# One core: the last two expert blocks in another order, second outputs fetched by adding gathers, and VectorE's order behind them

## Chip, cores and metric
One core of one Trainium2 chip. The metric is the device time of one execution in microseconds; the time of a kernel is the median of its runs.

## What is computed
One layer of a token mixer with a mixture-of-experts feed-forward on 512 latent tokens of width 2048 (and 256 context tokens). Only its last part matters here:

```
h   = rmsnorm(x2, norm2_w) * (1 + m4) + m3                # x2: tokens after the mixer
two experts of 16 per token, gates g0, g1, tokens sorted by expert into blocks of 128
y_b = (silu(h_b @ w1[e]) * (h_b @ w3[e])) @ w2[e]         # per block of 128 slots, times the gate
f[t]   = y[dest_0[t]] + y[dest_1[t]]
out[t] = rmsnorm(x2[t] + m5 * f[t], final_norm_w)
```

w1 and w3 are 2048 x 512 per expert, w2 is 512 x 2048.

## The kernel before, in words
All products are of float32 data, split into a high and a low part. A **unit** is half a 1 MB weight load: 128 x 1024 weights. For each unit ScalarE converts the high part (`e_hi`), VectorE subtracts it (`e_lo`), and TensorE makes six matmuls of 128 x 128 by 128 x 512 (`e_unit`, L1060 to L1070). Six raw buffers (`e_raw`) and six split ones (`e_hi`, `e_lo`) go round. Semaphore `e_units` counts finished units (six ahead), `e_split` the split ones, so ScalarE converts unit u when unit u-6 is done, and SyncE loads into a raw buffer when both its units are split (`load_e`, L621).

One block of the mixture has 24 units: eight up units for w1 into PSUM bank 0, eight for w3 into bank 1, eight down units for w2 into banks 2 to 5 (`up_unit`, `down_unit`). Between them stand the sigmoid (`sig1`, ScalarE), `silu` and `gate_up` (VectorE), four transposes of the gated activation (`turn_act`, TensorE) and the split of its transpose (`act_hi` on ScalarE, `act_lo` on VectorE, into `actT_hi` and `actT_lo`). The down products' result is scaled by the gates and copied to `y_sb` by ScalarE (`y_copy`, L1528), and GpSimd stores it in two halves into `block_outputs` in HBM (`store`, L2555 on).

The blocks are staggered: a turn of the loop makes the w1 units of block e, the w3 units of block e and the down units of block e-1. Blocks are numbered 0 to 15 (LAST = 15), and there were no extra blocks with these inputs. **The last turn** is written out by hand (L1137 to L1159): eight w1 units of block 15 (u = 0 to 7, with block 14's `turn_act` behind u = 2), eight down units of block 14 (u = 8 to 15), eight w3 units of block 15 (u = 16 to 23), then 16 small transposes, `turn_act(LAST)` and the eight down units of block 15 (u = 24 to 31). The list of loads (L642 on) and the loops of ScalarE (L1575 on) and VectorE (L2282 on) follow that order, each with the other work between chosen units. `AHEAD` is 5, so `u == AHEAD + 17` is u = 22. Block 15's outputs never go to HBM: ScalarE scales them into `v_last`, VectorE multiplies them by `m5_row`, and TensorE spreads them to their tokens by a one-hot matrix (`slots_last`) into PSUM. For token tiles 0 and 1 it first adds x2 there with an identity matrix (L1186), for tiles 2 and 3 a DMA adds x2 to `y_buf`.

**The outputs of blocks 0 to 14** come back by token: for each tile i of 128 tokens, `gather_y(z, i, ...)` (L2597) is an indirect DMA of 128 rows of 8 KB, z = 0 for the first expert of the token and z = 1 for the second. GpSimd issues them in this order once block 14's store has landed: (0,0) into `y_buf0`, (1,0) into `y_pair`, (0,1), (0,2), (0,3), then its own addition of `y_pair` into `y_buf0` (L2611), then the adding gathers (1,1), (1,2), (1,3), each behind the landing of its (0,i). Then it adds x2 of tiles 2 and 3 by DMA (L2620).

**VectorE's tail** (L2337 on) works on these: `modulate_y(i)` multiplies `y_buf i` by `m5_row`; `whole(i)` adds `y_buf i` and PSUM in two halves into x2; ScalarE then squares and sums the row (L1612); `finish(i)` takes the mean, waits for ScalarE's root, and multiplies by the reciprocal and `final_norm_w` (L2331). SyncE sends each tile out. The order is: four pieces of `v_last`, modulate 0, modulate 1, whole 0, modulate 2, modulate 3, whole 1, finish 0, finish 1, whole 2, whole 3, finish 2, finish 3.

Of the kernel before, what the change touches and what calls it, by code (L numbers as in the profile page):

```python
# [23 lines left out]
F32 = mybir.dt.float32  # L24
# [3 lines left out]
ALU = mybir.AluOpType  # L28
# [4 lines left out]
P = 128  # L33
D = 2048
# [3 lines left out]
NTOK = SEQ // P  # L38
NCTX = CTX // P
HEADS = 8  # L40
# [92 lines left out]
def build(nc, x, c, ctx_tokens, c_ctx, w_ada, b_ada, norm1_w, norm2_w, w_in, w_pool_group, pool_scale,  # L133
# [22 lines left out]
    with stack:  # L156
# [187 lines left out]
        y_buf = [Room(nc, base, at, at + 8).new(f"y_buf{i}", [P, D], F32) for i, at in enumerate((162, 98, 106, 10))]  # L344
        y_pair = Room(nc, base, 170, 178).new("y_pair", [P, D], F32)
        slots_last = Room(nc, base, 202, 204).new("slots_last", [P, NTOK, P], F32)
# [34 lines left out]
        def bank(b, n=512):  # L381
# [73 lines left out]
            [sem(f"y_in{i}") for i in range(NTOK)], sem("f_sum"), sem("o_rdy"), sem("o_out"))  # L455
        v_gated, v_out, slots_rdy, last_mm, y_mod, y_joined, USED = (
            c_sig_f, ff_taken, c_kgT_rdy, c_v_T, c_v_ev, c_kg_b, HEADS)
        y3_in, Y3_IN = rows_in, 7 * 16

# [53 lines left out]
        def _(sp):  # L513
# [112 lines left out]
            def piece(e, n):  # L626
                w, k, rows = (w_e1_d, n, 4) if n < 4 else (w_e3_d, n - 4, 4) if n < 8 else (w_e2_d, n - 8, 1)
                return w[ds(e, 1), :, rows * k:rows * k + rows, :].rearrange("o p k n -> (o p) (k n)")
# [16 lines left out]
            for i in range(16):  # L645
                load_e(L_LAST + i, (L_LAST + i) % EP,
                       piece(LAST - 1, 4 + i) if 4 <= i < 8 else piece(LAST, i if i < 4 else i - 4))
            sp.wait_ge(table_rdy, 1)
# [20 lines left out]
        def _(pe):  # L669
# [467 lines left out]
            pe.wait_ge(u_rdy, LAST)  # L1137
            for u in range(8):
                if u % 2 == 0:
                    pe.wait_ge(xe_rdy, LAST * 4 + (u // 2 + 3))  # L1140
                up_unit(G_LAST + u, (G_LAST + u) % EH, u, 0)
                if u == 2:
                    turn_act(LAST - 1)
            pe.wait_ge(actT_rdy, LAST + 2)
            pe.wait_ge(y_ev, LAST * 4)
            for u in range(8, 16):
                down_unit(G_LAST + u, (G_LAST + u) % EH, u - 8)
            pe.wait_ge(act_rdy, LAST)
# [50 lines left out]
        def _(act_e):  # L1199
# [375 lines left out]
            for u in range(AHEAD, 29):  # L1575
                last_hi(u)
                if u == AHEAD + 3:
                    act_hi(LAST - 1)
                if u == AHEAD + 9:
                    act_e.wait_ge(e_units, G_LAST + EH + 8)  # L1580
                    sig1(LAST)
                if u == AHEAD + 17:
                    y_copy(LAST - 1, LAST - 1, G_LAST + EH + 16)
            act_hi(LAST)
# [35 lines left out]
        def _(dve):  # L1620
# [661 lines left out]
            for u in range(AHEAD, 29):  # L2282
                last_lo(u)
                if u == AHEAD + 3:
                    act_lo(LAST - 1)
                if u == AHEAD + 9:
                    silu(LAST)
# [46 lines left out]
            def modulate_y(i):  # L2334
                tt(y_buf[i][:], y_buf[i][:], m5_row[:], ALU.mult).then_inc(y_mod, 1)

            for n in range(4):  # L2337
                cols = slice(n * 512, (n + 1) * 512)
                dve.wait_ge(v_gated, USED + n + 1)
                tt(v_last[:, cols], v_last[:, cols], m5_row[:, cols], ALU.mult).then_inc(v_out, 1)  # L2340
            dve.wait_ge(y_joined, USED + 1)
            modulate_y(0)
            dve.wait_ge(y_in[1], 16)
            modulate_y(1)
            dve.wait_ge(y_mod, USED + 1)
            whole(0)
            dve.wait_ge(y_in[2], 16)
            modulate_y(2)
            dve.wait_ge(y_in[3], 16)
            modulate_y(3)  # L2350
            dve.wait_ge(y_mod, USED + 2)
            whole(1)
            finish(0)
            finish(1)
            dve.wait_ge(y_in[2], 32)
            whole(2)
            dve.wait_ge(y_in[3], 32)
            whole(3)
            finish(2)
# [4 lines left out]
        def _(pool):  # L2364
# [238 lines left out]
            gather_y(0, 0, y_buf[0]).then_inc(y_in[0], 16)  # L2603
            gather_y(1, 0, y_pair).then_inc(y_in[0], 16)
            pool.wait_ge(e_split, 2 * EP + G_LAST + 24)
            gather_y(0, 1, y_buf[1]).then_inc(y0_in[0], 16)
            gather_y(0, 2, y_buf[2]).then_inc(y0_in[1], 16)
            pool.wait_ge(e_units, EH + G_LAST + 24)
            gather_y(0, 3, y_buf[3]).then_inc(y3_in, 16)
            pool.wait_ge(y_in[0], 32)  # L2610
            tt(y_buf[0][:], y_buf[0][:], y_pair[:], ALU.add).then_inc(y_joined, 1)  # L2611
            pool.wait_ge(y0_in[0], 16)
            gather_y(1, 1, y_buf[1], ALU.add).then_inc(y_in[1], 16)
            pool.wait_ge(y0_in[1], 16)
            gather_y(1, 2, y_buf[2], ALU.add).then_inc(y_in[2], 16)
            pool.wait_ge(y3_in, Y3_IN + 16)
            gather_y(1, 3, y_buf[3], ALU.add).then_inc(y_in[3], 16)
            for i in (2, 3):
# [57 lines left out]
```

## Time and profile before

| | |
|---|---|
| median of 3 runs | 2256.38 us (2256.22 to 2256.63) |
| the profiled execution | 2258.2 us |
| its span | 2256.6 us |
| mean granted clock of TensorE | 0.984 |
| busy: TensorE, VectorE, ScalarE, GpSimd | 96%, 69%, 44%, 24% |
| moved by DMA | 533.45 MB, mean 236 GB/s |

Times in the rows are microseconds from the start of the span, durations are microseconds too. A timeline row that merges several instructions (x4) gives the start of the first and their busy time together; in brackets stands how long the engine was idle before and what released it. The chain of waits follows the end of the program back to what released each step. PE is TensorE, DVE VectorE, ACT ScalarE, POOL GpSimd, SPq the DMA queue of SyncE, POOLq that of GpSimd.

### The profile page before, as it was taken

To read this page: it belongs to the slowest core of one execution; us is meant where nothing else is said; L and a number is where in the kernel's file an instruction comes from. 1 tells how busy PE (TensorE), PEld (TensorE's weight loads), DVE (VectorE), ACT (ScalarE), POOL (GpSimd) and SP (SyncE) were. 2 spreads that over 40 slices of the span, in tenths; PEclk is the share of its full clock that TensorE was granted. 3 is DMA by queue.
4 is the path that set the end of the run, shared out by engine and by line. 5 is a ranking of instruction groups with operands and counts; after the bars stand their busy time and mean duration, and the time that the engine had idled before them with its cause. 6 is when DMAs were issued, how large, how long until landed. Compare 5 with 4: busy or idle time off the path is not lost.

```text
span 2256.6 us, 36440 instructions
## 1 busy us (share of the span) xinstructions
PE 2162.3 (96%) x12376; PEld 1764.9 (78%) x12376; DVE 1552.2 (69%) x1941; ACT 992.4 (44%) x1216; POOL 536.3 (24%) x673
## 2 busy tenths in 40 slices
PE   4889999999999999999999999999799999999996
PEld 2679878888887887788888888788688888888883
DVE  3468555676567656766666766743688989889886
ACT  3334333333233324322222222332268888888882
POOL 0046435453554354111111111100000010110102
PEclk9989999999999999999999999999899999999998
DMA  9965462232222233677677666834499999999998
GB/s 388 390 208 156 149 217 79 85 93 80 83 86 84 83 89 96 214 225 248 213 226 248 218 222 207 273 128 148 171 385 407 416 415 421 417 418 418 418 377 258
DMA packets 327823, 533.45 MB, mean 236 GB/s; under 512 B 12464, under 2 KB 253616, under 8 KB 297808
## 3 DMA queue, kind: packets, MB, share of 16 engines
q1 hardware_dynamic: 294048, 393.91, 49.0%
q0 software_dynamic: 33712, 138.71, 17.6%
q8 instruction: 39, 0.64, 0.1%
q14 instruction: 24, 0.20, 0.0%
HBM read 493.74 MB, written 36.73 MB: 235 GB/s over the span
## 4 chain that ended last, share of the span: by engine, by line
PE 80%; DVE 4%; issue 2%; DMA 2%; POOL 1%; ACT 0%; DVEq 0%; POOLq 0%; ACTq 0%
PE ps L715 13%; PE ps L717 12%; PE ps L716 12%; PE ps L1070 7%; PE ps L1068 7%; PE ps L1069 7%; PE ps L946 3%; PE ps L947 3%; PE ps L948 3%; PE ps L1005 2%; PE ps L1007 2%; PE ps L1006 2%; PE ps L1094 1%; PE ps L825 1%; DMA y_buf<-block_outputs,dest_i 1%
## 5 line engine op out<-in xcount | busy, mean ns | idle before, releaser
L1666 DVE TENSOR_TENSOR w_lo<-raw,w_hi 128x1024 fp32r<-128x1024 f32 x272 | 349.1, 1283 | 357.1 <-ACT w_hi L1229 355.5
L1229 ACT CAST w_hi<-raw 128x1024 fp32r<-128x1024 f32 x272 | 285.1, 1048 | 584.6 <-PE ps L717 277.2
L715 PE MATMUL ps<-hl_hi,w_hi 128*128 128x512 f32 x1280 | 505.9, 395 | 3.6 <-DVE hl_lo L1732 1.4
L717 PE MATMUL ps<-hl_hi,w_lo 128*128 128x512 f32 x1280 | 498.8, 390 | 0.0
L716 PE MATMUL ps<-hl_lo,w_hi 128*128 128x512 f32 x1280 | 498.7, 390 | 0.0
L2121 DVE TENSOR_TENSOR e_lo<-e_raw,e_hi 128x1024 fp32r<-128x1024 f32 x357 | 421.5, 1220 | 44.1 <-ACT e_hi L1510 36.8
L1510 ACT CAST e_hi<-e_raw 128x1024 fp32r<-128x1024 f32 x357 | 369.1, 1058 | 72.6 <-PE ps L1070 72.4
L715 PEld LDWEIGHTS ps<-hl_hi,w_hi 128*128 128x128 f32 x1280 | 240.4, 188 | 54.7 <-issue 3.4
L717 PEld LDWEIGHTS ps<-hl_hi,w_lo 128*128 128x128 f32 x1280 | 240.3, 188 | 50.8
L716 PEld LDWEIGHTS ps<-hl_lo,w_hi 128*128 128x128 f32 x1280 | 240.5, 188 | 47.8
L1068 PE MATMUL ps<-e_hi,xe_hi 128*128 128x512 f32 x512 | 201.2, 393 | 0.1
L1070 PE MATMUL ps<-e_hi,xe_lo 128*128 128x512 f32 x512 | 199.5, 390 | 0.0
L1069 PE MATMUL ps<-e_lo,xe_hi 128*128 128x512 f32 x512 | 199.3, 389 | 0.0
L1952 DVE SCALAR_TENSOR_TENSOR ada_acc<-ada,silu_c,ada_acc 128x512 f32<-128x512 f32 x240 | 180.2, 751 | 12.1 <-DMA ada<-in_w_ada 5.3
L2559 POOL DMA_DIRECT2D block_outputs<-y_sb x30 | 16.2, 540 | 467.7 <-ACT y_sb L1533 460.9
L1070 PEld LDWEIGHTS ps<-e_hi,xe_lo 128*128 128x128 f32 x512 | 96.1, 188 | 20.3
L1068 PEld LDWEIGHTS ps<-e_hi,xe_hi 128*128 128x128 f32 x512 | 96.4, 188 | 19.5 <-DVE xe_lo L2225 0.3
L1069 PEld LDWEIGHTS ps<-e_lo,xe_hi 128*128 128x128 f32 x512 | 96.2, 188 | 19.4
L1068 PE MATMUL ps<-e_hi,actT_hi 128*128 128x512 f32 x256 | 105.4, 412 | 1.4 <-DVE actT_lo L2244 1.4
L1005 PE MATMUL ps<-w_hi,m_hi 128*128 128x512 f32 x256 | 100.7, 393 | 1.6 <-DVE m_lo L1971 1.6
L1070 PE MATMUL ps<-e_hi,actT_lo 128*128 128x512 f32 x256 | 101.4, 396 | 0.0
L1069 PE MATMUL ps<-e_lo,actT_hi 128*128 128x512 f32 x256 | 100.6, 393 | 0.0
(388 smaller groups left out, 3588.5 us busy)
## 6 DMA issues: line engine op xcount, KB each, us to landing
e_raw<-in_w_e SPq DMA_DIRECT2D x192, 1024.0 KB, 9.6
raw<-in_w_in SPq DMA_DIRECT2D x208, 512.0 KB, 3.9
ada<-in_w_ada POOLq DMA_DIRECT2D x64, 1024.0 KB, 6.4
ada_ring<-in_w_ada SPq DMA_DIRECT2D x32, 1024.0 KB, 14.2
raw<-in_w_out SPq DMA_DIRECT2D x32, 512.0 KB, 4.0
block_outputs<-y_sb POOLq DMA_DIRECT2D x30, 512.0 KB, 6.7
block_outputs<-osq POOLq DMA_DIRECT2D x1, 8192.0 KB, 27.8
raw<-in_w_branch_hgrn SPq DMA_DIRECT2D x16, 512.0 KB, 3.8
```

The lines of the kernel that those rows point to most:

```text
L715: mm(dst, hi, rhs_hi[:, k, :], start=(k == 0), stop=False)
L716: mm(dst, hi, rhs_lo[:, k, :], start=False, stop=False)
L717: last = mm(dst, lo, rhs_hi[:, k, :], start=False, stop=(k == KT - 1))
L1005: mm(bank(t), a_hi, hi, start=(k == 0), stop=False)
L1068: mm(bank(b), a_hi, hi, start=start, stop=False)
L1069: mm(bank(b), a_hi, lo, start=False, stop=False)
L1070: last = mm(bank(b), a_lo, hi, start=False, stop=stop)
L1229: act_e.copy(w_hi[:, hslot, :], raw[:, slot, :]).then_inc(hi_done, 1)
L1510: act_e.copy(e_hi[:, n % EH, :], e_raw[slot][:, n % 2, :]).then_inc(e_hi_done, 1)
L1666: tt(w_lo[:, hslot, :], raw[:, slot, :], w_hi[:, hslot, :].bitcast(F32), ALU.subtract).then_inc(split_done, 1)
L1952: ins = stt(out=acc[:], in0=w, scalar=cs[:, 0, k:k + 1], in1=acc[:], op0=ALU.mult, op1=ALU.add)
L2121: tt(e_lo[:, n % EH, :], e_raw[n // 2 % EP][:, n % 2, :], e_hi[:, n % EH, :].bitcast(F32), ALU.subtract).then_inc(e_split, 1)
```

## The change
In the last turn the down units of block 14 stand between the two halves of block 15's w1 units: u = 0 to 3 are w1, u = 4 to 11 down, u = 12 to 15 w1, and the rest is as before. `turn_act(14)` follows u = 0; loads, conversions, the copy to `y_sb` and the sigmoid are moved accordingly. The pair buffer and GpSimd's addition go: every second output is added by its gather, (1,0) behind the landing of (0,0) and ahead of (0,3). VectorE multiplies `y_buf0` before `v_last`, modulate 2 comes before whole 0, and the order behind the last gather is modulate 3, finish 0, whole 1, finish 1. Two semaphores less are used for the gathers.

```diff
@@ -342,7 +342,6 @@
         fn_row = Room(nc, base, 194, 202).new("fn_row", [P, D], F32)
 
         y_buf = [Room(nc, base, at, at + 8).new(f"y_buf{i}", [P, D], F32) for i, at in enumerate((162, 98, 106, 10))]
-        y_pair = Room(nc, base, 170, 178).new("y_pair", [P, D], F32)
         slots_last = Room(nc, base, 202, 204).new("slots_last", [P, NTOK, P], F32)
         f_junk = Room(nc, base, 42, 50).new("f_junk", [P, D], F32)
 
@@ -453,9 +452,7 @@
 
         y_in, f_sum, o_rdy, o_out = (
             [sem(f"y_in{i}") for i in range(NTOK)], sem("f_sum"), sem("o_rdy"), sem("o_out"))
-        v_gated, v_out, slots_rdy, last_mm, y_mod, y_joined, USED = (
-            c_sig_f, ff_taken, c_kgT_rdy, c_v_T, c_v_ev, c_kg_b, HEADS)
-        y3_in, Y3_IN = rows_in, 7 * 16
+        v_gated, v_out, slots_rdy, last_mm, y_mod, USED = c_sig_f, ff_taken, c_kgT_rdy, c_v_T, c_v_ev, HEADS
 
         block = stack.enter_context(nc.Block())
 
@@ -644,7 +641,7 @@
                     load_e(e * 12 + (n - 4), (n + 2) % EP, piece(e, n) if n < 8 else piece(e - 1, n))
             for i in range(16):
                 load_e(L_LAST + i, (L_LAST + i) % EP,
-                       piece(LAST - 1, 4 + i) if 4 <= i < 8 else piece(LAST, i if i < 4 else i - 4))
+                       piece(LAST - 1, 6 + i) if 2 <= i < 6 else piece(LAST, i if i < 2 else i - 4))
             sp.wait_ge(table_rdy, 1)
             n_extra = sp.value_load(route_i[0:1, 7:8], min_val=0, max_val=NXTRA)
             with sp.Fori(0, NXTRA) as b:
@@ -1135,16 +1132,19 @@
                     if 17 <= q <= 20:
                         turn_x(e + 1, q - 17)
             pe.wait_ge(u_rdy, LAST)
-            for u in range(8):
-                if u % 2 == 0:
-                    pe.wait_ge(xe_rdy, LAST * 4 + (u // 2 + 3))
-                up_unit(G_LAST + u, (G_LAST + u) % EH, u, 0)
-                if u == 2:
+            for u in range(16):
+                if u in (0, 2, 12, 14):
+                    pe.wait_ge(xe_rdy, LAST * 4 + ((u if u < 4 else u - 8) // 2 + 3))
+                if u == 4:
+                    pe.wait_ge(actT_rdy, LAST + 2)
+                    pe.wait_ge(y_ev, LAST * 4)
+                if 4 <= u < 12:
+                    down_unit(G_LAST + u, (G_LAST + u) % EH, u - 4)
+                else:
+                    up_unit(G_LAST + u, (G_LAST + u) % EH, u if u < 4 else u - 8, 0)
+                if u == 0:
+                    pe.wait_ge(xe_rdy, LAST * 4 + 5)
                     turn_act(LAST - 1)
-            pe.wait_ge(actT_rdy, LAST + 2)
-            pe.wait_ge(y_ev, LAST * 4)
-            for u in range(8, 16):
-                down_unit(G_LAST + u, (G_LAST + u) % EH, u - 8)
             pe.wait_ge(act_rdy, LAST)
             for u in range(16, 24):
                 up_unit(G_LAST + u, (G_LAST + u) % EH, u - 16, 1)
@@ -1574,13 +1574,13 @@
 
             for u in range(AHEAD, 29):
                 last_hi(u)
-                if u == AHEAD + 3:
+                if u == AHEAD + 1:
                     act_hi(LAST - 1)
-                if u == AHEAD + 9:
-                    act_e.wait_ge(e_units, G_LAST + EH + 8)
+                if u == AHEAD + 13:
+                    y_copy(LAST - 1, LAST - 1, G_LAST + EH + 12)
+                if u == AHEAD + 17:
+                    act_e.wait_ge(e_units, G_LAST + EH + 16)
                     sig1(LAST)
-                if u == AHEAD + 17:
-                    y_copy(LAST - 1, LAST - 1, G_LAST + EH + 16)
             act_hi(LAST)
             for u in range(29, 32):
                 last_hi(u)
@@ -2281,9 +2281,9 @@
 
             for u in range(AHEAD, 29):
                 last_lo(u)
-                if u == AHEAD + 3:
+                if u == AHEAD + 1:
                     act_lo(LAST - 1)
-                if u == AHEAD + 9:
+                if u == AHEAD + 17:
                     silu(LAST)
             gate_up(LAST, G_LAST + EH + 24)
             own.wait()
@@ -2334,28 +2334,26 @@
             def modulate_y(i):
                 tt(y_buf[i][:], y_buf[i][:], m5_row[:], ALU.mult).then_inc(y_mod, 1)
 
+            dve.wait_ge(y_in[0], 32)
+            modulate_y(0)
             for n in range(4):
                 cols = slice(n * 512, (n + 1) * 512)
                 dve.wait_ge(v_gated, USED + n + 1)
                 tt(v_last[:, cols], v_last[:, cols], m5_row[:, cols], ALU.mult).then_inc(v_out, 1)
-            dve.wait_ge(y_joined, USED + 1)
-            modulate_y(0)
-            dve.wait_ge(y_in[1], 16)
-            modulate_y(1)
+            for i in (1, 2):
+                dve.wait_ge(y_in[i], 32)
+                modulate_y(i)
             dve.wait_ge(y_mod, USED + 1)
             whole(0)
-            dve.wait_ge(y_in[2], 16)
-            modulate_y(2)
-            dve.wait_ge(y_in[3], 16)
+            dve.wait_ge(y_in[3], 32)
             modulate_y(3)
+            finish(0)
             dve.wait_ge(y_mod, USED + 2)
             whole(1)
-            finish(0)
             finish(1)
-            dve.wait_ge(y_in[2], 32)
-            whole(2)
-            dve.wait_ge(y_in[3], 32)
-            whole(3)
+            for i in (2, 3):
+                dve.wait_ge(y_in[i], 48)
+                whole(i)
             finish(2)
             finish(3)
 
@@ -2601,20 +2599,16 @@
 
             pool.wait_ge(xe_T, 4 * E)
             gather_y(0, 0, y_buf[0]).then_inc(y_in[0], 16)
-            gather_y(1, 0, y_pair).then_inc(y_in[0], 16)
             pool.wait_ge(e_split, 2 * EP + G_LAST + 24)
-            gather_y(0, 1, y_buf[1]).then_inc(y0_in[0], 16)
-            gather_y(0, 2, y_buf[2]).then_inc(y0_in[1], 16)
+            gather_y(0, 1, y_buf[1]).then_inc(y_in[1], 16)
+            gather_y(0, 2, y_buf[2]).then_inc(y_in[2], 16)
+            pool.wait_ge(y_in[0], 16)
+            gather_y(1, 0, y_buf[0], ALU.add).then_inc(y_in[0], 16)
             pool.wait_ge(e_units, EH + G_LAST + 24)
-            gather_y(0, 3, y_buf[3]).then_inc(y3_in, 16)
-            pool.wait_ge(y_in[0], 32)
-            tt(y_buf[0][:], y_buf[0][:], y_pair[:], ALU.add).then_inc(y_joined, 1)
-            pool.wait_ge(y0_in[0], 16)
-            gather_y(1, 1, y_buf[1], ALU.add).then_inc(y_in[1], 16)
-            pool.wait_ge(y0_in[1], 16)
-            gather_y(1, 2, y_buf[2], ALU.add).then_inc(y_in[2], 16)
-            pool.wait_ge(y3_in, Y3_IN + 16)
-            gather_y(1, 3, y_buf[3], ALU.add).then_inc(y_in[3], 16)
+            gather_y(0, 3, y_buf[3]).then_inc(y_in[3], 16)
+            for i in range(1, NTOK):
+                pool.wait_ge(y_in[i], 16)
+                gather_y(1, i, y_buf[i], ALU.add).then_inc(y_in[i], 16)
             for i in (2, 3):
                 pool.wait_ge(y_mod, USED + i + 1)
                 pool.dma_start(y_buf[i][:], x2[:, i, :], accum_op=ALU.add).then_inc(y_in[i], 16)
```

## Rows read from the trace of the kernel before

**Rows 1.** The page, part 1: busy time of each engine.
```profile
PE 2162.3 (96%) x12376; PEld 1764.9 (78%) x12376; DVE 1552.2 (69%) x1941; ACT 992.4 (44%) x1216; POOL 536.3 (24%) x673
```

**Rows 2.** Chain of waits, 2184 to 2257: start, us, what.
```profile
2190.22 6.12 DMA block_outputs<-y_sb
...
2198.96 8.48 DMA y_pair<-block_outputs,dest_i
...
2207.52 4.60 POOL y_buf L2611
...
2216.08 15.89 DMA y_buf<-block_outputs,dest_i
```

**Rows 3.** Transfers issued at 2096, 2166, 2185, 2196.6, 2203.2, 2212.3, 2234.6, 2249: us to landing.
```profile
block_outputs<-y_sb POOLq DMA_DIRECT2D x1, 512.0 KB, 8.1
...
block_outputs<-y_sb POOLq DMA_DIRECT2D x1, 512.0 KB, 9.1
...
e_raw<-in_w_e SPq DMA_DIRECT2D x1, 1024.0 KB, 9.0
...
y_buf<-block_outputs,dest_i POOLq DMA_INDIRECT x1, 6.7
...
y_buf<-block_outputs,dest_i POOLq DMA_INDIRECT x1, 11.7
...
y_buf<-block_outputs,dest_i POOLq DMA_INDIRECT x1, 9.0
...
y_buf<-x POOLq DMA_DIRECT2D x1, 1024.0 KB, 7.3
...
out<-x SPq DMA_DIRECT2D x1, 1024.0 KB, 3.9
```

**Rows 4.** Timeline of GpSimd: start, us, instruction, idle before.
```profile
2196.61 2.05 POOL L2598 DMA_INDIRECT y_buf<-block_outputs,dest_i  x1 [5.85 <-DMA block_outputs<-y_sb]
...
2203.15 0.94 POOL L2598 DMA_INDIRECT y_buf<-block_outputs,dest_i  x1 [0.30 <-issue]
...
2212.27 1.61 POOL L2598 DMA_INDIRECT y_buf<-block_outputs,dest_i  x1 [0.16 <-issue]
```

**Rows 5.** Stages: PE, PEld, DVE, ACT, POOL busy, granted clock, DMA share, GB/s.
```profile
2127.00:2162.00 35.00, 35.00 (x166) 29.22 (x165) 31.87 (x32) 29.66 (x35) 2.97 (x4) 1.00 1.01 418
...
2201.00:2204.00 3.00, 3.00 (x9) 2.33 (x8) 1.03 (x1) 0.64 (x1) 2.39 (x3) 0.50 0.98 347
...
2219.00:2222.00 3.00, 3.00 (x8) 1.33 (x7) 0.70 (x1) 0.95 (x2) 0.13 (x1) 1.00 1.03 213
```

**Rows 6.** Timeline of TensorE.
```profile
2162.67 0.39 PE L1068 MATMUL ps<-e_hi,xe_hi 128*128 128x512 f32 x1
...
2184.95 0.39 PE L1068 MATMUL ps<-e_hi,xe_hi 128*128 128x512 f32 x1
...
2219.09 3.60 PE L1193 MATMUL ps<-v_last,slots_last 128*128 128x512 f32 x8
...
2235.47 5.18 PE L1193 MATMUL ps<-v_last,slots_last 128*128 128x512 f32 x8 [2.49 <-DVE x L2319]
```

**Rows 7.** Timeline of ScalarE.
```profile
2165.44 3.90 ACT L1573 CAST e_hi<-e_raw 128x1024 fp32r<-128x1024 f32 x4
...
2187.51 2.42 ACT L1533 ACTIVATE y_sb<-ps,gate_tab 128x512 f32<-128x512 f32 x4
...
2236.75 1.89 ACT L1612 ACTIVATE f_junk<-x 128x2048 f32<-128x2048 f32 x1
```

**Rows 8.** Timeline of VectorE.
```profile
2166.54 4.63 DVE L2279 TENSOR_TENSOR e_lo<-e_raw,e_hi 128x1024 fp32r<-128x1024 f32 x4 [2.71 <-ACT e_hi L1573]
...
2223.51 2.35 DVE L2319 TENSOR_TENSOR x<-y_buf,ps 128x1024 f32<-128x1024 f32 x2
...
2234.20 2.34 DVE L2319 TENSOR_TENSOR x<-y_buf,ps 128x1024 f32<-128x1024 f32 x2
...
2242.23 4.61 DVE L2319 TENSOR_TENSOR x<-y_buf,ps 128x1024 f32<-128x1024 f32 x4
```

## Prediction, made before the changed kernel was seen

> **What bounds the kernel now.** I read the page first: TensorE is busy for 96% of the span [rows 1], so up to the last turn its own products set the time. The chain of waits of the last 70 us says where that ends: TensorE leads to ScalarE's copy of block 14's outputs, and from there to the end the chain never touches TensorE. It is store (ends 2196.3), pair of gathers (second lands 2207.4), GpSimd's sum of the pair (4.6 us), adding gathers (last lands 2231.97), then VectorE [rows 2]. So the tail is bound by block 14's way through HBM and by the order on VectorE behind the gather that comes last. Block 15's products run beside this; their slack is worked out in part 3.
>
> How fast the queue works is in the issues and GpSimd's timeline [rows 3, 4]. Plain gathers: token tile 0 lands at 2196.61 + 6.7 = 2203.3, the pair's second at 2207.4 (4.1 later), three more by 2203.15 + 11.7 = 2214.85, so 2.47 each. Adding gathers: the first lands at 2212.27 + 9.0 = 2221.3, the third at 2231.97, so 5.35 each; the stages show why they are the dear ones: the DMA engines are full both times, but move 418 GB/s in the steady loop and 213 among the adding gathers [rows 5].
>
> **Part 1, TensorE's order.** The work is the same, in another order. A turn's first sixteen units and four transposes take 2184.95 - 2162.67 = 22.3 us, 1.36 a unit [rows 6]. The down products of block 14 end after unit 11 in place of unit 15, 5.4 us earlier. But they now begin at unit 4 and need actT_lo of block 14. ScalarE comes out of block 13's copy with a backlog, its four conversions start at 2165.44 and run back to back [rows 7], and VectorE's four subtractions from 2166.54 take 4.63, with actT_lo behind them at 2171.1 [rows 8]. Now two stand ahead: actT_lo starts at 2166.54 + 2.3 = 2168.8 and ends 0.7 later at 2169.5; TensorE would want it at 2162.67 + 4 x 1.36 + 0.45 = 2168.6. That is a new stall of 0.95 us. The copy (2187.51 before [rows 7]) keeps its place one conversion behind the unit, so it starts 5.4 - 0.95 = 4.5 earlier, at 2183.0, and the stores are issued at 2184.6 and 2185.7 (2189.1 and 2190.22 before).
>
> **Part 2, the store.** The second half took 6.1 us [rows 2], issued when the weight loads were ending. 4.5 us earlier it shares full DMA engines, as in the loop, where second halves took 8.1 and 9.1 [rows 3]. Bounds: 6.1 and 9.1. I take 7.6, between them, because fewer loads are outstanding than in the loop: it lands at 2193.3, 3.0 us earlier. The two halves there needed over 9 us together, about a quarter of what the engines moved.
> The Trainium skill (DMA: Bandwidth & Descriptors, Queues, rings and completion order) says that each DMA engine takes turns between the queues that have work, a packet at a time; by that rule the store would land earlier than I take, and the time would be 2253.8. The loop's rows speak against it.
>
> **Part 3, the load order.** Sixteen 1 MB loads as before, in the order of the products. The copy now stands between the conversions of units 18 and 19, and the last load waits for unit 19's split: it ends at about 2187.8, where the load was issued at 2185. It lands 3.9 (an idle 1 MB transfer) to 9.0 us later [rows 3], 2191.7 to 2196.8, and ScalarE can use it from 2194.3. So block 15's gate may come up to 2.5 us later, on top of 0.95. This I cost at nothing: token tile 0's products ended at 2219.09 + 3.6 = 2222.7 [rows 6], with both delays 2226.2, and the new order wants them at 2227.7 (below). Without that cover it costs what it runs over. The later sigmoid and silu also cost nothing: they follow unit 15 by two units, and gate_up needs them behind unit 23.
>
> **Part 4, GpSimd and its queue.** The sum on GpSimd goes (4.6 us, plus a gap before the adding gathers of 2221.3 - 5.35 - 2214.85 = 1.1), and a plain gather becomes an adding one. Nothing has to wait for an empty queue: when (1,0) is issued, right behind the landing of (0,0), two plain gathers are still under way. From the first landing to the last: before 2231.97 - 2203.3 = 28.7. After 4.1 + 2.47 + 2.47 + 4 x 5.35 = 30.4. That is 1.8 more. The saved gap and sum are smaller than the added transfer, because the sum mostly ran beside plain gathers. Bounds for an adding gather in its new places: 4.9, twice a plain one, and 6.45, the first with its gap (2221.3 - 2214.85): -1.6 to +4.4 over four.
> First landing: 3.0 earlier, 2200.3. Token tile 3's second output: 2230.8, 1.2 earlier. Others: y_in 0 at 2212.3, y_in 1 at 2220.1, y_in 2 at 2225.4.
>
> **Part 5, VectorE.** modulate_y(0) moves ahead of the v_last pieces. It runs 2212.3 to 2214.6, v_last follows by 2217.2. Their reader starts at 2219.09 [rows 6]: no cost. whole(0) now stands behind modulate_y(2), and so at 2227.7 where it was at 2223.51 [rows 8]. The square of tile 0 is done by 2232.1, before finish(0) wants it: no cost.
> Then the place where it costs. Call the last gather's landing T. Before: modulate_y(3) at T, whole(1) at T + 2.2, finish(0), finish(1), whole(2) at 2242.23 = T + 10.26 [rows 8]. finish(0) lay between whole(1) and finish(1) and hid ScalarE's square of tile 1 (1.9 [rows 7], and 0.2 to read the sum). After: modulate_y(3) 2.2, finish(0) 2.9, whole(1) 2.35, then finish(1) finds nothing to do until the square: 0.1 + 2.0 exposed and 0.15 of steps; then 2.9. whole(2) starts at T + 12.55. **2.3 us more behind T.** Two other arrivals lie close: tile 3's products start behind whole(1)'s first half, T + 6.4, and took 5.2 [rows 6], T + 11.6; the adding of x2 tile 3 lands at T + 2.6 + 7.3 = T + 9.9 [rows 3]. whole(3) wants both at T + 14.8: nothing.
> From whole(2) on nothing changes.
>
> **Sum.** -3.0 (store) + 1.8 (queue) + 2.3 (VectorE) = +1.1 us. whole(2) 2243.35 for 2242.23. The profiled execution took 2258.2 (span 2256.6), 1.8 over the median of the runs; its 2259.3 becomes 2257.5 against the median of 2256.38. About 0.2% (4.5 us) is what a measurement of this kernel can tell from no change.
>
> **Rivals.**
> *The adding is free.* If an adding gather costs little more than a plain one in a queue that is already full, the queue's term is 1.8 - 2.9 = -1.1, and the time 2254.6. For: the first of the three had a restart in it. Against: 213 GB/s at full engines over three windows [rows 5]. 0.08.
> *Equal turns for the store.* If the store gets half of the 418 GB/s [rows 5] from its first issue, its 1.05 MB are down 5 us later, at 2189.6, 3.7 earlier than I take: 2253.8. For: two queues on the same engines. Against: the loop's 8.1 and 9.1. 0.08. The two rivals together would give 2250.9, the only way I see to a gain of over 0.2%; with what I overlook, 0.08.
> *The queue clogs (the other side).* Place: four adding gathers with a plain one between them and the addition of x2 tile 2 behind. Price: 6.45 each, as the first took, +4.4, so 2261.9. It is slower by over 0.2% from 6.2 an adding gather on. For: that row. Against: the following two took 5.35 on the mean. 0.12, with a store of 9.1 us on top of smaller excesses.
> *The stall lowers the clock.* Behind the pauses ahead of block 15's down products the granted clock is 0.50, 1.2 GHz, and nine matmuls take 3 us instead of 2 [rows 5]. If the stall of 0.95 does that in the last turn, the store comes 1 to 2 us later: 2259.3. Against: there the engine had done only small transposes around its pauses, here it is full before and after. 0.07.
> *The change doesn't do what it says*, because ScalarE is still behind when the copy is due. But four conversions take 3.9 us beside four units' 5.4 [rows 6, 7], so the 2.4 of block 13's copy are made up within seven units, and the new copy stands at unit 12. Under 0.02, counted within no change.
>
> **Chances.** The forecast case 0.65, its own range 2255.5 to 2259.5 (store 6.1 to 8.6, adding gathers 5.0 to 5.7). With the free adding, the equal turns and the clock 0.80 for within 0.2%, 0.08 for faster, 0.12 for slower. The range reaches to the rivals at 2254.6 and most of the way to the clogged queue: 2254.2 to 2261.0.
>
> **What would show it.** On TensorE a pause near 1 us before unit 4, on ScalarE the copy at about 2183, a second store of 7 to 8 us, GpSimd's sum gone; four adding gathers of 5.3 us, the last landing near 2231; on VectorE an idle stretch of 2 us before finish(1), with ScalarE's square as its releaser, and whole(2) some 12.5 us behind the last gather. A last gather before 2228, or finish(1) without that wait, makes the forecast wrong.

## Result, and the profile after

| | before | changed |
|---|---|---|
| median of the runs | 2257.99 us (22 runs) | 2261.35 us (22 runs) |
| ratio, 95% interval | | 1.0015, 1.0009 to 1.0021 |
| profiled execution, its span | 2258.2, 2256.6 us | 2258.68, 2257.1 us |
| a second profile, its span | 2257.24, 2255.5 us | 2259.86, 2258.2 us |

The changed kernel is slower by 3.4 us, interval 2.0 to 4.7 us. That is 0.15%, below the 0.2% of the prediction. One of its 22 executions took 3579.55 us; the ratio leaves it out, and without it the median is 2261.26. Two things have to be kept apart. Over 22 runs the kernel before has a median 1.6 us above that of the three runs shown. And single executions of one program differ by several us (before: 2253.3 to 2260.5), since the place at which the last turn begins moves: 2162.67 and 2162.18 in the two profiles of before, 2161.00 and 2162.82 in those of the changed kernel, and 2160.41 (f) to 2165.18 (i) over all profiles here, although all these kernels do the same work up to there. The spans of two profiles therefore say little; the tails, from that place to the end, say more. All times "from the turn" below are counted from the first product of the last turn, 2162.67 in the first profile of before [rows 6] (in the others 0.48 us ahead of ScalarE's copy of block 13, as there).

The page of the changed kernel, span and busy times:

```profile
span 2257.1 us, 36440 instructions
...
PE 2160.4 (96%) x12376; PEld 1763.0 (78%) x12376; DVE 1552.6 (69%) x1941; ACT 992.9 (44%) x1216; POOL 530.5 (24%) x672
```

TensorE does the same 12376 matmuls. The chain of waits from the last turn on (start, us, what):

```profile
2181.47 0.36 ACT y_sb L1533
...
2186.17 7.89 DMA e_raw<-in_w_e
...
2202.24 13.48 DMA y_buf<-block_outputs,dest_i
...
2215.98 14.29 DMA y_buf<-block_outputs,dest_i
...
2233.28 2.10 issue
...
2237.76 2.01 ACT f_junk L1612 x2
```

The chain still starts at ScalarE's copy of block 14, now 6.0 us earlier on the clock and 4.4 earlier from the turn (20.47 for 24.84). But then it goes through a weight load that lands late (2194.06), and from there over block 15's gate and down products to the issue of gather (0,3) at 2202.24. That issue is no price by itself: the queue was full, and in experiment a the same gather was issued 0.3 us later from the turn and took 12.4 us to land in place of 13.5. At the end there are two new pieces: 2.10 us ahead of whole(1), in which VectorE runs the multiplication of finish(0), and ScalarE's square of tile 1, 2.01 us, which nothing covers. (finish(0) would have run somewhere in any case; the square is what is added.) The last gather lands at 2215.98 + 14.29 = 2230.27.

The store's second half and the last weight load, us to landing:

```profile
block_outputs<-y_sb POOLq DMA_DIRECT2D x1, 512.0 KB, 9.8
...
e_raw<-in_w_e SPq DMA_DIRECT2D x1, 1024.0 KB, 7.9
```

and the stages beside them (busy time of PE, PEld, DVE, ACT, POOL, then granted clock, DMA share, GB/s):

```profile
2186.00:2190.00 4.00, 4.00 (x19) 3.31 (x18) 4.00 (x5) 4.00 (x5) 0.00 (x0) 1.00 1.02 406
...
2190.00:2194.00 4.00, 4.00 (x19) 3.33 (x18) 4.00 (x5) 2.14 (x3) 0.00 (x0) 1.00 0.59 246
...
2194.00:2197.00 3.00, 3.00 (x23) 2.61 (x21) 2.46 (x3) 2.00 (x2) 2.45 (x2) 1.00 0.26 71
...
2218.00:2221.00 3.00, 3.00 (x8) 1.33 (x7) 0.50 (x1) 0.41 (x2) 0.00 (x0) 1.00 1.05 218
```

The store took 9.8 us for 6.1 before [rows 2] and landed at 2194.0, in the same moment as the last weight load (2186.17 + 7.89). That load was issued 25.17 us from the turn and landed at 33.06, where before it was issued at 22.27 and landed at 31.3 [rows 3], 2.4 us ahead of the store. From 2190 on the DMA engines were busy only 59% of the time and moved 246 GB/s. Among the adding gathers (the last row) they move 218 GB/s at full share, as before [rows 5].

The packets of the two queues show how the store went, q0 being GpSimd's queue and q1 SyncE's (packets, MB, share of the engines; the first pair of rows is 2187 to 2189, the second 2191 to 2193.6):

```profile
q0 software_dynamic: 167, 0.63, 84.4%
q1 hardware_dynamic: 30, 0.15, 17.8%
...
q1 hardware_dynamic: 77, 0.50, 46.6%
q0 software_dynamic: 18, 0.05, 5.1%
```

The store's first half was issued at 2183.03, and the first packet of either half began 3.7 us later, at 2186.7. By 2191 all but 0.05 MB of the 1.05 MB had moved. The last 5% then took until 2193.5, beside the packets of the last load. Before, the first packet began 1.7 us behind the first issue.

GpSimd (start, us, instruction, idle before it):

```profile
2184.18 0.53 POOL L2557 DMA_DIRECT2D block_outputs<-y_sb  x1 [0.62 <-ACT y_sb L1533]
...
2194.25 1.24 POOL L2596 DMA_INDIRECT y_buf<-block_outputs,dest_i  x1 [9.53 <-DMA block_outputs<-y_sb]
...
2200.32 1.61 POOL L2596 DMA_INDIRECT y_buf<-block_outputs,dest_i  x1 [1.84 <-DMA y_buf<-block_outputs,dest_i]
...
2215.98 1.54 POOL L2596 DMA_INDIRECT y_buf<-block_outputs,dest_i  x1 [6.99 <-DMA y_buf<-block_outputs,dest_i]
```

The first gather starts at 2194.25, 33.25 from the turn. Before it was 33.94. TensorE and VectorE at the places of the prediction:

```profile
2167.88 0.50 PE L1065 MATMUL ps<-e_hi,actT_hi 128*128 128x512 f32 x1 [0.77 <-DVE actT_lo L2244]
```

```profile
2167.15 0.68 DVE L2244 TENSOR_TENSOR actT_lo<-ps,actT_hi 128x512 fp32r<-128x512 f32 x1
...
2230.29 2.29 DVE L2335 TENSOR_TENSOR y_buf<-y_buf,m_row 128x2048 f32<-128x2048 f32 x1 [0.35 <-DMA y_buf<-block_outputs,dest_i]
...
2235.38 2.34 DVE L2319 TENSOR_TENSOR x<-y_buf,ps 128x1024 f32<-128x1024 f32 x2
...
2239.84 0.15 DVE L2325 TENSOR_SCALAR stat<-stat 128x1 f32<-128x1 f32 x1 [2.11 <-ACTq L1614]
...
2242.73 4.61 DVE L2319 TENSOR_TENSOR x<-y_buf,ps 128x1024 f32<-128x1024 f32 x4
```

TensorE's stall ahead of unit 4 is 0.77 us, released by actT_lo as forecast, with no fall of the clock (granted clock 1.00). VectorE runs modulate_y(3) at 2230.29 right behind the last gather, whole(1) at 2235.38, then 2.11 us of nothing ahead of finish(1), released by ScalarE's queue, and whole(2) at 2242.73, 12.46 behind the gather. Before it was 10.26 [rows 8].

From the turn, in us, for all kernels that ran (a to i are the experiments below):

| kernel | store's 2nd half lands | first gather lands | last gather lands | whole(2) | end | ratio of times, interval |
|---|---|---|---|---|---|---|
| before | 33.67 | 40.64 | 69.31 | 79.56 | 93.93 | |
| before, again | 33.57 | | 68.74 | 78.99 | 93.32 | |
| changed | 32.98 | 39.05 | 69.28 | 81.73 | 96.10 | 1.0015, 1.0009 to 1.0021 |
| changed, again | 33.13 | 38.94 | 68.60 | 81.05 | 95.38 | |
| a: VectorE's order back | 33.39 | 39.39 | 68.68 | 78.91 | 93.28 | 1.0006, 0.9997 to 1.0015 |
| b: before, VectorE's order alone | 33.36 | | 68.26 | 80.77 | 95.16 | 1.0012, 1.0003 to 1.0021 |
| c: gathers alone | 33.15 | 39.44 | 68.67 | 78.90 | 93.31 | 0.9995, 0.9986 to 1.0004 |
| d: turn's order alone | 33.70 | | 69.15 | 80.44 | 94.90 | 1.0002, 0.9993 to 1.0011 |
| e: small last loads (7/8 of units 20 to 31 left out) | 26.49 | 32.98 | 64.34 | 76.78 | 91.12 | one run |
| f: two pair buffers | | | 65.12 | 78.08 | 92.59 | 0.9995, 0.9986 to 1.0004 |
| g: f with the turn's order | | 39.56 | 64.01 | 76.43 | 91.07 | 0.9998, 0.9988 to 1.0008 |
| h: store ahead of last loads | before 28.2 | 38.24 | 66.78 | 77.00 | 91.33 | 0.9995, 0.9986 to 1.0004 |
| i: gate earlier alone | | 38.78 | 67.81 | 78.04 | 92.42 | 0.9998, 0.9989 to 1.0007 |

Where a cell is empty the trace has no landing for that transfer. The landings are good to about 0.05 us. Two profiles of one program differ by 0.6 to 0.7 in the last two columns of times; smaller differences are no finding.

### The profile page after: what moved, and what is told of

It is laid out like the page before. It is cut to its first block, busy times and chain, and to the rows that moved or that the text cites. A ratio compares the mean times of both kernels' runs of the same rounds, so it can differ in the third digit from the quotient of the medians.

```text
span 2257.1 us, 36440 instructions
## 1 busy us (share of the span) xinstructions
PE 2160.4 (96%) x12376; PEld 1763.0 (78%) x12376; DVE 1552.6 (69%) x1941; ACT 992.9 (44%) x1216; POOL 530.5 (24%) x672
## 4 chain that ended last, share of the span: by engine, by line
PE 80%; DVE 4%; DMA 2%; issue 2%; ACT 1%; POOL 1%; DVEq 0%; ACTq 0%; POOLq 0%; SPq 0%
PE ps L712 13%; PE ps L714 12%; PE ps L713 12%; PE ps L1065 7%; PE ps L1067 7%; PE ps L1066 7%; PE ps L943 3%; PE ps L944 3%; PE ps L945 3%; PE ps L1002 2%; PE ps L1004 2%; PE ps L1003 2%; DMA y_buf<-block_outputs,dest_i 1%; PE ps L1091 1%; PE ps L822 1%
## 5 line engine op out<-in xcount | busy, mean ns | idle before, releaser
L1067 PEld LDWEIGHTS ps<-e_hi,xe_lo 128*128 128x128 f32 x512 | 96.1, 188 | 20.3
```

The source lines that it names most:

```text
L1067: last = mm(bank(b), a_lo, hi, start=False, stop=stop)
```

## Experiments

### a. The changed kernel with VectorE's order of before

```diff
             modulate_y(3)
-            finish(0)
             dve.wait_ge(y_mod, USED + 2)
             whole(1)
+            finish(0)
             finish(1)
```

> The changed kernel with VectorE's order behind the last gather put back (modulate 3, whole 1, finish 0, finish 1). Theory 1 (the exposed square of tile 1 is what slows it): whole(2) starts 10.3 us behind the last gather in place of 12.45, no idle stretch before finish(1), time 2.2 us below the changed kernel, equal to before within 1 us. Theory 2 (the queue is what slows it): the order gives back under 1 us, the time stays 2 to 3 us above before. Theory 3 (TensorE's new order costs): likewise above before.

VectorE behind the last gather:

```profile
2231.49 2.29 DVE L2335 TENSOR_TENSOR y_buf<-y_buf,m_row 128x2048 f32<-128x2048 f32 x1 [0.34 <-DMA y_buf<-block_outputs,dest_i]
...
2233.70 2.35 DVE L2319 TENSOR_TENSOR x<-y_buf,ps 128x1024 f32<-128x1024 f32 x2
...
2236.57 2.35 DVE L2331 SCALAR_TENSOR_TENSOR x<-x,stat,fn_row 128x2048 f32<-128x2048 f32 x1
...
2239.46 2.35 DVE L2331 SCALAR_TENSOR_TENSOR x<-x,stat,fn_row 128x2048 f32<-128x2048 f32 x1
...
2241.73 4.61 DVE L2319 TENSOR_TENSOR x<-y_buf,ps 128x1024 f32<-128x1024 f32 x4
```

whole(1) follows modulate_y(3), finish(0) covers the square, and whole(2) is 10.23 behind the gather. The end is 2.8 and 2.1 us earlier from the turn than in the two profiles of the changed kernel, and the ratio goes from 1.0015 to 1.0006, 2.0 us. The two intervals overlap (1.0009 to 1.0021, 0.9997 to 1.0015), so the times alone don't prove the step; the tail does. Theory 1 holds; 2 and 3 would have left the tail and the time where they were.

### b. The kernel before with finish(0) ahead of whole(1)

```diff
+            finish(0)
             dve.wait_ge(y_mod, USED + 2)
             whole(1)
-            finish(0)
             finish(1)
```

> The kernel before with finish(0) put ahead of whole(1), nothing else. Theory 1: whole(2) starts 12.5 us behind the last gather in place of 10.26, time 2.2 us above before. Theory 2: less than 1 us, since a last gather at the same place leaves the queue's part unchanged and VectorE has room.

```profile
2232.16 2.29 DVE L2335 TENSOR_TENSOR y_buf<-y_buf,m_row 128x2048 f32<-128x2048 f32 x1 [0.69 <-DMA y_buf<-block_outputs,dest_i]
...
2237.26 2.35 DVE L2319 TENSOR_TENSOR x<-y_buf,ps 128x1024 f32<-128x1024 f32 x2
...
2241.72 0.15 DVE L2325 TENSOR_SCALAR stat<-stat 128x1 f32<-128x1 f32 x1 [2.11 <-ACTq L1614]
...
2244.61 4.61 DVE L2319 TENSOR_TENSOR x<-y_buf,ps 128x1024 f32<-128x1024 f32 x4
```

The same 2.11 us of idle time appear ahead of finish(1), and whole(2) is 12.5 behind the gather. The time is 1.0012 of before, 2.7 us, interval 0.7 to 4.7. One line moved alone gives 2.7 of the whole change's 3.4 us, as far as such intervals tell. Theory 1 again.

### c. The gathers alone

```diff
 # last turn on all engines and VectorE's tail in the order of before
-            gather_y(1, 0, y_pair).then_inc(y_in[0], 16)
+            gather_y(1, 0, y_buf[0], ALU.add).then_inc(y_in[0], 16)
-            tt(y_buf[0][:], y_buf[0][:], y_pair[:], ALU.add).then_inc(y_joined, 1)
```

> The changed kernel with the last turn's order of before on all engines and VectorE's tail in the order of before; only the gathers differ from before (second output of tile 0 by an adding gather, no sum on GpSimd). Theory 1, with the queue's term as the trace after shows it (29.95 us from the first landing to the last for 28.7): time 1.3 us above before, the last gather 1.3 later from the start of the last turn. Theory 2: 3 us or more above before.

The forecast 1.3 us do not come: the interval of the ratio ends at 0.9 us above before. The way from the first landing to the last does get longer, 68.67 - 39.44 = 29.23 for 28.67, but by 0.6, and the last gather lands where it does in the second profile of before. The trace shows something that I had not priced: what the sum on GpSimd did to VectorE. In the second profile of before, GpSimd and VectorE:

```profile
2205.51 4.60 POOL L2611 TENSOR_TENSOR y_buf<-y_buf,y_pair 128x2048 f32<-128x2048 f32 x1 [3.15 <-DMA y_pair<-block_outputs,dest_i]
```

```profile
2205.89 5.30 DVE L2279 TENSOR_TENSOR e_lo<-e_raw,e_hi 128x1024 fp32r<-128x1024 f32 x1 [0.83 <-ACT e_hi L1573]
...
2224.83 1.22 DVE L2319 TENSOR_TENSOR x<-y_buf,ps 128x1024 f32<-128x1024 f32 x1 [1.44 <-PE ps L1193]
```

VectorE's subtraction of the last unit, 1.23 us everywhere else, takes 5.30. It meets GpSimd's sum, which began 0.4 us earlier, and ends 1.1 us behind it, about its own length. TensorE gets the unit late, and whole(0) waits for its products (1.44 and 0.44 us idle, released by TensorE). The same is seen in b and f (5.20 us) and in d (6.23 us for a row of two, 5.09 of it the first). In the first profile of before the sum started at 2207.52 [rows 2], 1.1 us after that subtraction, which took 1.23, and so I did not see it. In g the subtraction had also begun first, by 0.03 us, and there it was the sum that took longer, 5.66 us for 4.60:

```profile
2205.45 5.66 POOL L2616 TENSOR_TENSOR y_buf<-y_buf,y_pair 128x2048 f32<-128x2048 f32 x1 [1.98 <-DMA y_pair<-block_outputs,dest_i]
```

In c, without the sum:

```profile
2205.70 1.23 DVE L2276 TENSOR_TENSOR e_lo<-e_raw,e_hi 128x1024 fp32r<-128x1024 f32 x1 [1.02 <-ACT e_hi L1570]
...
2222.97 2.34 DVE L2316 TENSOR_TENSOR x<-y_buf,ps 128x1024 f32<-128x1024 f32 x2
...
2230.65 2.29 DVE L2332 TENSOR_TENSOR y_buf<-y_buf,m_row 128x2048 f32<-128x2048 f32 x1 [2.62 <-DMA y_buf<-block_outputs,dest_i]
```

Here the last subtraction takes 1.23 and whole(0) starts at 60.98 from the turn, for 62.65 in the second profile of before. But this does not reach the end: VectorE waits for the last gather in both (2.62 us idle here, 1.02 in the second profile of before), and whole(2) starts 10.23 and 10.25 behind it. That the last gather is not later has another reason: the first one landed at 39.44 for 40.64, 0.7 quicker behind its issue and 0.5 for an earlier store, which makes up for the 0.6. The time, 0.9995, can't be told from no change. Theory 2 is out.

### d. The order of the last turn alone

```diff
 # loads, TensorE, ScalarE and VectorE's splits of the last turn from the change; gathers and tail as before
-            for u in range(8):
-                    turn_act(LAST - 1)
+                if 4 <= u < 12:
+                    down_unit(G_LAST + u, (G_LAST + u) % EH, u - 4)
```

> The kernel before with the new order of the last turn alone (TensorE, ScalarE, VectorE's splits, loads). Theory 1, with the store held by the loads as after (9.8 us for its second half): the stall of 0.8 us before unit 4, the store landing 0.7 earlier from the start of the last turn, everything behind it 0.7 earlier, time 0.7 us below before. Theory 3: the stall or the late last load costs, time above before. If the store should land 3 us earlier as I forecast, the time is 3 us below before.

The store's second half, us to landing:

```profile
block_outputs<-y_sb POOLq DMA_DIRECT2D x1, 512.0 KB, 10.5
```

It is issued 4.4 us earlier and lands at 33.70 from the turn, where it did before. Nothing of the earlier copy is left. The ratio of 1.0002 bears neither a gain of 3 us nor a loss of more than 2.5. The end at 94.90 is 1.0 to 1.6 above before, in an execution that has the blocked subtraction (6.23 us for two):

```profile
2227.81 1.22 DVE L2322 TENSOR_TENSOR x<-y_buf,ps 128x1024 f32<-128x1024 f32 x1 [4.24 <-PE ps L1196]
```

whole(0) waits 4.24 us for TensorE, starts at 65.01 from the turn for 62.65 in the second profile of before, and VectorE comes to modulate_y(3) 0.85 us behind the last gather. whole(2) is 11.29 behind it for 10.26, so 1.0 us is lost there. With one profile I can't say how much of that the order adds and how much the blocked subtraction.

### e. The changed kernel with small last loads

```diff
+            def load_part(n, slot, src):                      # 256 of 2048 columns
             for i in range(16):
-                load_e(
+                (load_e if i < 10 else load_part)(
```

> The changed kernel with the last six weight loads cut to an eighth of their columns (what they leave out is 7/8 of the weights of units 20 to 31, so block 15's outputs are not the reference's). Theory A (the store is held by the weight loads it now runs beside): the second half of block 14's store takes 5 to 6 us in place of 9.8, lands at 29 us from the start of the last turn in place of 33.0, and all gathers follow 3 to 4 us earlier. Theory B (GpSimd's queue itself is slow, whatever the loads do): 8 to 10 us as in the changed kernel.

```profile
block_outputs<-y_sb POOLq DMA_DIRECT2D x1, 512.0 KB, 3.3
```

```profile
2178.00:2186.00 8.00, 8.00 (x37) 6.60 (x36) 7.13 (x6) 6.71 (x8) 0.00 (x0) 1.00 0.24 75
```

The kernel leaves out 7/8 of the weights of units 20 to 31, so it does not compute the layer; it is run for the traffic alone. With the loads out of the way (75 GB/s from 2178 to 2186 for the usual 418) the same half store takes 3.3 us and lands at 26.5 from the turn. The last gather follows at 64.34, 4.9 and 4.3 earlier than in the two profiles of the changed kernel. Theory A: the store is held by the weight loads.

### f and g. A second pair buffer, with either order of the last turn

```diff
+        y_pair1 = Room(nc, base, 18, 26).new("y_pair1", [P, D], F32)
             gather_y(0, 3, y_buf[3]).then_inc(y3_in, 16)
+            gather_y(1, 1, y_pair1).then_inc(y0_in[0], 16)
             pool.wait_ge(y_in[0], 32)
             tt(y_buf[0][:], y_buf[0][:], y_pair[:], ALU.add).then_inc(y_joined, 1)
-            gather_y(1, 1, y_buf[1], ALU.add).then_inc(y_in[1], 16)
+            # behind the issue of (1, 2) and (1, 3)
+            tt(y_buf[1][:], y_buf[1][:], y_pair1[:], ALU.add).then_inc(y_joined, 1)
```

> The kernel before with the second output of tile 1 fetched plain as well, into a second pair buffer, summed by GpSimd behind the issue of the last two adding gathers: six plain gathers and two adding ones. If an adding gather costs the queue 5.3 us and a plain one 2.5, and the queue has no gap ahead of the adding ones, the last gather lands 3 to 4 us earlier from the start of the last turn (65.5 for 68.3 to 69.3), and the time is 3 us below before. If the adding gathers cost no more than plain ones beside others, less than 1 us. If TensorE's products of token tile 1 (done at 66.9 us) or GpSimd's second sum become the bound, 1 to 2 us.

> The same with the new order of the last turn on top. If the store lands where it did whatever the order (33.0 to 33.7 us), and block 15's products come later, no gain over the version with the order of before, up to 1.5 us slower. If the earlier store pays once the queue is shorter, 1 to 3 us faster than it.

The queue does what its prices say: the last gather lands at 65.12 and 64.01, 3.6 to 5.3 earlier than in before. In f the end gains only 0.7 to 1.3 of that: whole(0) again waits for TensorE behind a blocked subtraction (5.20 us), and VectorE comes late to the last tiles (whole(2) 12.96 behind the last gather). In g, where the subtraction escaped the sum (2.58 for two), whole(0) starts at 61.74 for 62.65 and the end is 91.07. The measured times are 0.9995 and 0.9998 of before, 1.1 and 0.5 us less, with intervals of -3.2 to +0.9 and -2.7 to +1.8 us. That fits the 0.7 to 1.3 of f's profile. The 2.3 to 2.9 of g's lie at the far end of its interval. The runs can tell neither from no change; the 3 us forecast for f come neither in its tail nor in its median.

### h and i. The store ahead of the last two loads, and its control

```diff
 # both against the changed kernel, and both with whole(1) ahead of finish(0) as in a
+                if i == 14:
+                    sp.wait_ge(y_out, 16 * (2 * LAST + NTOK))   # in h alone
                 load_e(L_LAST + i, ...
-            for u in range(AHEAD, 29):                          # ScalarE and VectorE
+            for u in range(AHEAD, 26):
-            for u in range(29, 32):
+            for u in range(26, 32):
```

> The changed kernel with VectorE's order of before behind the last gather, the last two weight loads issued only when block 14's store has landed, and block 15's gate and its transpose ahead of the conversions of units 26 to 31. If the store was held by those loads, its second half takes 4 to 6 us in place of 9.8 to 10.2, lands at 28 to 29 us from the start of the last turn, the last gather lands at 64 to 65 for 68.7, and the time is 3 to 4 us below before. If the late loads hold TensorE's down products of block 15 instead, whole(0) waits for TensorE and the time is within 1 us of before.

> The same without SyncE's wait: only VectorE's order of before and the earlier gate of block 15. Block 15's gate comes 1 to 2 us earlier, but the gathers do not, and the tail hangs on them: the time stays within 1 us of before, and 3 us above the version with the wait if the store is what counts.

GpSimd of h, and its stages (columns as above):

```profile
2187.15 0.53 POOL L2559 DMA_DIRECT2D block_outputs<-y_sb  x1 [0.63 <-ACT y_sb L1535]
...
2192.21 1.10 POOL L2598 DMA_INDIRECT y_buf<-block_outputs,dest_i  x1 [4.53 <-DMA block_outputs<-y_sb]
...
2202.45 2.44 POOL L2598 DMA_INDIRECT y_buf<-block_outputs,dest_i  x1 [5.04 <-DMA y_buf<-block_outputs,dest_i]
```

```profile
2190.00:2194.00 4.00, 4.00 (x19) 3.31 (x18) 4.00 (x5) 4.00 (x5) 1.10 (x1) 1.00 0.31 77
...
2194.00:2198.00 4.00, 4.00 (x20) 3.30 (x19) 2.45 (x3) 0.06 (x1) 2.65 (x2) 1.00 1.02 426
...
2198.00:2202.00 4.00, 2.60 (x23) 2.32 (x21) 2.17 (x6) 1.38 (x2) 0.00 (x0) 1.00 1.01 426
```

The store is down when the first gather is issued at 28.24 from the turn, 5.0 earlier than in the changed kernel and at the time forecast (28 to 29), so two loads were enough to hold it. But the loads put off then run at 426 GB/s from 2194 to 2202, on top of the first gathers, and the first of these takes 10.0 us and lands only 0.7 to 0.8 earlier. The last lands at 66.78, 1.9 earlier than in a, but not at the forecast 64 to 65. The traffic is moved, not removed. The end is 2.0 earlier than in a. The time is 0.9995 of before, 1.1 us less with an interval of -3.2 to +0.9: it can't be told from before, nor from i (0.9998), and it neither shows nor excludes what the tail gained.

### The two kernels again

> The kernel before, for a second profile: what differs from the first between two executions of the same program. Any part of the tail that moves by over 0.5 us here is no finding in the others. I expect the stores within 0.3 us and the landing of the last gather within 1 us of 69.3.

> The changed kernel for a second profile. I expect the store's second half at 9 to 10.5 us again, the last gather within 1 us of 69.3 from the start of the last turn, whole(2) 12.45 behind it, and the end at 95.2 to 96.2; the kernel before had 93.93 and 93.32 in two profiles.

Both came as in the table: the tail of before ends at 93.3 and 93.9, that of the changed kernel at 95.4 and 96.1. The difference of the tails is 2.1 to 2.2 us in each pair, at the lower edge of the interval of the runs (2.0 to 4.7). Whether the remaining 1.2 us are more than chance I can't say; no part of the tail shows them.

## Why the prediction was right or wrong

- **Part 1, TensorE's order.** Right. The stall is 0.77 us (0.95 forecast), with the cause named, and the copy starts 4.4 us earlier (4.5). The rival of a lower clock is out: the granted clock stayed at 1.00.
- **Part 2, the store. This term failed.** "I take 7.6, between them, because fewer loads are outstanding than in the loop: it lands at 2193.3, 3.0 us earlier." It took 9.8 and 10.0, above the upper bound of 9.1, and landed 0.4 to 0.7 earlier. The reason given for 7.6 was wrong too: when the second half was issued, 23.2 us from the turn, two loads were under way (issued at 17.8 and 20.6) and a third followed 2.0 us later; in the loop, at 3.6 from the turn, two were under way (-3.7 and -0.1) and a third followed 1.5 us later. No fewer were outstanding. Before the change the last load had landed 2.4 us ahead of the store; now it lands with it, at 33.1. d shows the same without the rest of the change (33.70), e and h show what the store is without the loads (3.3 us in e, down 5 us earlier in h). So it is the loads that hold it, and the rival of equal turns, which had the store down 5 us behind its first issue, is out as a forecast: it took 11. The Trainium skill (DMA: Bandwidth & Descriptors, Queues, rings and completion order) says that an engine goes from queue to queue packet by packet. The trace doesn't speak against that: from 2187 to 2189 the store had 84% of the engines, and from 2189 to 2191 the store moved 89 packets and the loads 69. The rule alone doesn't give the landing, which was set by a start 3.7 us behind the issue and by the last 5% of the bytes. Why the start and those last packets are so late, while the engines are busy only 59% in the last 4 us, stays open.
- **Part 3, the load order.** Right in kind: the last load was issued late and used late (ScalarE idle 1.6 us for it), and its cover held; whole(0) never waited for TensorE in the changed kernel. Without that cover, in d, it waited 4.24 us.
- **Part 4, the queue.** Forecast +1.8; from the first landing to the last it took 30.23 and 29.66 for 28.67, +1.0 to +1.6, and the first gather was quicker behind its issue by 0.9 to 1.2. That it came near the forecast is luck in part: the last three adding gathers landed 4.8 to 4.9 behind the gather ahead of them, not 5.35, and the plain ones behind the first took 3.0 to 3.8 each and not 4.1 and 2.47. That adding gathers move half of what plain ones do was right (218 GB/s at full engines), so the rival of free adding is out, and none took 6 us or more, so the clogged queue is too. The step "the sum mostly ran beside plain gathers" was true of the queue, but the sum blocked VectorE in most executions; in before that cost the end nothing, in d and f a part of it reached the end.
- Parts 2 and 4 together: the last gather 1.2 earlier was forecast, 0.0 to 0.1 is what it is (69.28 for 69.31, 68.60 for 68.74).
- **Part 5, VectorE.** Right. 2.2 us more behind the last gather, where 2.3 was forecast: 12.45 for 10.26, with the idle 2.11 us in front of finish(1), and shown from both sides by a and b.
- **The number.** The sum gave +1.1, the tails +2.1, the runs +3.4. I forecast no change that can be told, and a loss of 0.15% was measured: below my 0.2%, but with an interval that leaves out zero. The time of 2261.35 lies 0.35 above the range, and 3.85 above the 2257.5 of the sum. Of these, 1.0 us is the tail: the store gave 2.3 to 2.6 less than forecast, and the quicker first gather (0.9 to 1.2) and the smaller excess of the queue (0.2 to 0.8) happened to hide more than half of it. 1.6 us is that the three runs shown stood below the median of 22, which the range made no room for. The other 1.2 us no part of the tail shows.

## What to carry to other kernels

The store that was moved 4.4 us earlier into saturated load traffic landed with the loads, not with its issue: before counting on such a move, look for the moment when the load traffic ends. Where a wait on a second engine (here ScalarE's square, 2.1 us) is covered by one instruction between producer and consumer, moving that instruction away cost the whole wait; when ordering a serial tail, alternate the tiles. An elementwise sum on GpSimd is not free beside VectorE: look at how long VectorE's instructions take while it runs, in more than one profile, and whether the engine had time to spare there. And take the median of more than three runs when a forecast of 1 us is to be checked: it moved by 1.6 us here.

## What was not expected of the hardware

- A VectorE subtraction of 128 x 1024 took 5.1 to 5.3 us in place of 1.23 when GpSimd's 4.6 us sum of float32 tiles had begun 0.4 to 0.6 us ahead of it, and ended 1.1 us behind the sum, in four of six executions that had the sum (before again, b, d, f). In the other two, before and g, the subtraction had begun first and took 1.23; in g, where the sum began 0.03 us behind it, the sum took 5.66. That the sum blocks it is read from these coincidences and from c; it was not tried by itself. The Trainium skill (SBUF — State Buffer, SBUF: two separate sides) states just this: a GpSimd instruction that reads SBUF and a VectorE instruction with two SBUF inputs contend for one pair of ports, which whichever starts first holds for its whole length while the other is blocked. The traces agree: blocked for about the rest of the sum, then its own 1.2 us, and in g the sum longer by about the subtraction's length. It was a rule that spoke for the change, and the prediction did not weigh it.
- The second half megabyte of block 14's store took 3.3 us with little other traffic, 5.6 to 6.1 where the loads were ending, and 9.8 to 10.5 where the last loads were still running. Of the 11.0 us from the first half's issue to the landing in the changed kernel, 3.7 passed ahead of the first packet, and the last 5% of the bytes took 2.5.
- Adding gathers of 1 MB lie 4.8 to 5.8 us apart at 213 to 218 GB/s, plain ones 2.5 us among themselves and 3.0 to 3.8 where adding ones stand between them; f and g gained 3.6 to 5.3 us at the last gather by turning one adding gather of three into a plain one and closing the gap ahead of them.
